# NSA compression: cached tokens transposed by VectorE in 32x32 blocks, from pages fetched in quarters

## What is computed

```python
chunks = kv_pad[:, :, :2].reshape(b, n_chunks, CMP_STRIDE, 2, NSA_KV_HEADS, NSA_HEAD_DIM)   # CMP_STRIDE 16
w1 = w1.reshape(2, CMP_LEN, NSA_HEAD_DIM, CMP_HIDDEN)                                      # 2, 32, 64, 128
pos_bias = jnp.einsum('rld,rlde->re', cmp_pos, w1)
pa = jnp.einsum('bnlrkd,rlde->bnrke', chunks, w1[:, :CMP_STRIDE])
pb = jnp.einsum('bnlrkd,rlde->bnrke', chunks, w1[:, CMP_STRIDE:])
hidden = jax.nn.gelu(pa[:, :-1] + pb[:, 1:] + pos_bias[:, None, :])
out = jnp.einsum('bnrke,ref->bnrkf', hidden, w2)
```

## Time and profile before

| | before |
|---|---|
| median of 3 runs | 2550.19 us (2540.56 to 2556.83) |
| profiled execution, span of the trace | 2552.3 us |
| TensorE busy | 2406.9 us, 94% |
| VectorE busy | 1308.8 us, 51% |
| ScalarE busy | 735.5 us, 29% |
| POOL busy | 26.4 us, 1% |
| share of the 16 DMA engines, SP's queue | 54.8% |

### The profile page before, as it was taken

The page is one execution under the profiler, slowest core; times in us unless marked ns, Lnnn a source line. Parts: engine busy times, 40 slices in busy tenths (PEclk is TensorE's granted clock), DMA queues, the critical chain, the costliest instruction groups (busy, mean ns, idle before and its releaser), DMA issues. The chain is left out here.

```text
span 2552.3 us, 45434 instructions
## 1 busy us (share of the span) xinstructions
PE 2406.9 (94%) x19182; PEld 2040.0 (80%) x19182; DVE 1308.8 (51%) x2332; ACT 735.5 (29%) x1763; POOL 26.4 (1%) x26
## 2 busy tenths in 40 slices
PE   8989988899999889999999898999999998979998
PEld 6668865699986767999888766899985786648998
DVE  2257384265552373666443285366631865535565
ACT  2125373221022342210232293221021445522200
POOL 0000000000000010000000010000000000000000
PEclk9999899999999979999999857999999997889999
DMA  9997616965644317666433255656671865293440
GB/s 346 307 241 166 210 49 214 350 229 213 245 160 144 99 56 283 212 251 223 154 132 134 68 150 195 233 204 256 217 207 66 181 177 159 71 321 122 172 170 22
DMA packets 287343, 472.71 MB, mean 185 GB/s; under 512 B 14956, under 2 KB 105149, under 8 KB 286662
## 3 DMA queue, kind: packets, MB, share of 16 engines
q1 hardware_dynamic: 272370, 456.04, 54.8%
q10 hardware_dynamic: 14770, 13.76, 1.7%
HBM read 448.72 MB, written 38.04 MB: 191 GB/s over the span
## 5 line engine op out<-in xcount | busy, mean ns | idle before, releaser
L631 PE MATMUL PS<-hT,ring 128*128 128x132 f32 x2048 | 249.7, 277 | 6.6 <-DVE hT L756 4.2
L631 PEld LDWEIGHTS PS<-hT,ring 128*128 128x128 f32 x2048 | 238.3, 190 | 11.9 <-issue 11.2
L631 PE MATMUL PS<-mT,arena 128*128 128x132 f32 x1536 | 184.6, 276 | 0.0
L631 PEld LDWEIGHTS PS<-mT,arena 128*128 128x128 f32 x1536 | 178.7, 190 | 0.0
L2687 PE MATMUL PS<-hT,ring 128*128 128x264 f32 x768 | 172.7, 386 | 0.1
L2687 PEld LDWEIGHTS PS<-hT,ring 128*128 128x128 f32 x768 | 145.1, 190 | 24.9 <-issue 0.4
L768 DVE TENSOR_TENSOR arena<-arena,PS 128x264 f32<-128x264 f32 x224 | 89.7, 427 | 130.8 <-PE PS L631 129.6
L715 ACT ACTIVATE arena<-arena 128x528 f32<-128x528 f32 x64 | 41.1, 642 | 312.1 <-DVE arena L768 312.1
L631 PE MATMUL PS<-arena,ring 128*128 128x132 f32 x1024 | 126.9, 277 | 0.0
L631 PE MATMUL PS<-hT,arena 128*128 128x132 f32 x1024 | 125.7, 276 | 0.0
L631 PE MATMUL PS<-mT,ring 128*128 128x132 f32 x1024 | 125.7, 276 | 0.0
(11 more groups left out here) (490 smaller groups left out, 4364.0 us busy)
## 6 DMA issues: line engine op xcount, KB each, us to landing
arena<-in_w_ada SPq DMA_DIRECT2D x36, 2048.0 KB, 12.1
ring<-in_w_mlp_in SPq DMA_DIRECT2D x32, 2048.0 KB, 8.7
ring<-in_w_mlp_out SPq DMA_DIRECT2D x32, 2048.0 KB, 8.1
ring<-in_w_ada SPq DMA_DIRECT2D x12, 2048.0 KB, 19.9
ring<-in_ssd_w_in SPq DMA_DIRECT2D x12, 2048.0 KB, 7.9
ring<-in_nsa_w_in SPq DMA_DIRECT2D x10, 2048.0 KB, 9.5
arena<-in_cache_nsa_kv SPq DMA_DIRECT2D x64, 256.0 KB, 10.5
ring<-in_cache_nsa_kv SPq DMA_DIRECT2D x64, 256.0 KB, 8.0
```

Of the source, the lines that this page charges most:

```text
L631: ins = nc.tensor.matmul(PS[:, bank, at:at + HALF], lhs[:, k, p * 128:(p + 1) * 128], rhs[:, k, :], start=opens and k == 0, stop=closes an ...
```

## The change

The cached tokens are no longer transposed by TensorE through PSUM but by VectorE within SBUF: one instruction transposes 128x1024 numbers in blocks of 32x32 (L1463 in the kernel after). Such a transposition moves numbers only inside a quarter of 32 partitions, so the tokens have to lie in other places. A page is now fetched in four transfers: quarter i takes the tokens 8c + 2i and 8c + 2i + 1 (c from 0 to 15) to the partitions 32i + 16(q mod 2) onwards, 16 neighbouring partitions with two places of 2 KB in each (`quarter_pages`). A group is 64 transfers of 64 KB instead of 16 of 256 KB. SP issues those of 12 pages (48) and POOL those of 4 (16); of group 0 POOL issues all 64, in the input projection and behind the wait for the sample's hidden state (`h_sample`). The buffers are one tile of 16 x 512 numbers a partition each.

The two differences become one instruction of 128x1024 into `delta`, with the odd chunk read twice and the even chunk read at two offsets. The weights lie in the same new order: `w1[0]` and `w1[1]` come in 16 transfers of 32 partitions each (`compress_weights`), and the table of positions in four instead of one. The result of the third product alternates between banks 2 and 4. ScalarE has no copies of cached tokens any more. TensorE's transposes and both copies are gone for all ten products: the prompt's rows go the same way, by four transfers of 32 partitions. The semaphores for transposed data are called `turned` (VectorE done) and `product_made` (TensorE done with `x[:, j]`).

```diff
-            slots = [ring[:, (st["used"] + 2 + i) % SLOTS, :, :] for i in range(2)]
-            return [[P(CMP // 2, 2 * KV * HD) for _ in range(2)], slots]
-
-        def chunk_pages(sp, L, g, G, samples=(0, 1)):
-
-
-            for b in samples:
-                for n in range(0, PAGES, 4):
-                    numbers = page_numbers(sp, [(2 * g + b) * PAGES + q for q in range(n, n + 4)])
-                    for q, number in zip(range(n, n + 4), numbers):
-                        page = cache_chunks[bass.ds(number + L * N_PHYS, 1), :, :, 0:2, :]
-                        fetched[g % 2].on(sp.dma_start(G[g % 2][b][q:128:PAGES],
-                                                       page.rearrange("g c t r n -> (g c) t (r n)")), 16)
+            return [P(2 * PAGES, 2 * KV * HD), ring[:, 0:2].rearrange("p s k n -> p (s k) n")]
+
+        def quarter_pages(engine, kind, signals_, L, g, G, items):
+
+
+            for n in range(0, len(items), 2):
+                b, q0 = items[n]
+                numbers = page_numbers(engine, [(2 * g + b) * PAGES + q for _b, q in items[n:n + 2]], kind)
+                for number, (b, q) in zip(numbers, items[n:n + 2]):
+                    for i in range(4):
+                        part = cache_quarters[bass.ds(number + L * N_PHYS, 1), i, :, :, 0:2, :]
+                        row = 32 * i + 16 * (q % 2)
+                        signals_[g % 2].on(engine.dma_start(G[g % 2][row:row + 16, 8 * b + q // 2 * 2:8 * b + q // 2 * 2 + 2, :],
+                                                            part.rearrange("g c t r n -> (g c) t (r n)")), 16)
+
+        POOL_PAGES = [(1, q) for q in range(4, PAGES)]
+        SYNC_PAGES = [(0, q) for q in range(PAGES)] + [(1, q) for q in range(4)]
+
+        def sync_pages(sp, L, g, G):
+            quarter_pages(sp, mybir.EngineType.SP, fetched, L, g, G, SYNC_PAGES)
+
+        def pool_pages(gp, L, g, G):
+            quarter_pages(gp, mybir.EngineType.Pool, fetched_pool, L, g, G, POOL_PAGES)
+
+        def compress_weights(sp, done, dst, L, r):
+
+            src = a["nsa_cmp_w1"][L, r].rearrange("(h i c d) e -> i d h c e", h=4, i=4, c=4)
+            to = dst.rearrange("p (h c e) -> p h c e", h=4, c=4)
+            for h in range(4):
+                for i in range(4):
+                    done.on(sp.dma_start(to[32 * i:32 * i + 32, h], src[i, :, h]), 16)
...
-                loaded2.on(sp.dma_start(mT_flat[:, 0:2048].rearrange("p (j e) -> p j e", j=16),
-                                        a["nsa_cmp_w1"][L, 0].rearrange("(j p) e -> p j e", p=128)), 16)
-                if first:
-                    chunk_pages(sp, L, 0, G, (0,))
-                    issue(sp, n0 + 11)
-                    chunk_pages(sp, L, 0, G, (1,))
-                    issue(sp, n0 + 13)
-                else:
-                    chunk_pages(sp, L, 0, G)
-                    issue(sp, n0 + 5)
+                compress_weights(sp, loaded2, mT_flat[:, 0:2048], L, 0)
+                issue(sp, n0 + (13 if first else 5))
...
+            def gp_part(gp):
+                gp.wait_ge(h.h_sample.sem, h.h_sample.at(1))
+                quarter_pages(gp, mybir.EngineType.Pool, fetched_pool, L, 0, G, SYNC_PAGES + POOL_PAGES)
...
+            def pair_bank(n):
+
+                return PS[:, (2, 4)[n % 2], 0:256]
...
+            def rows_of(buffer, r, j):
+
+
+                return buffer.rearrange("p (y t) (r k h d) -> p t r h k y d", t=2, r=2, k=KV, h=2)[:, j // 2, r, j % 2]
+
+            def columns_of(j):
+
+
+                return x[:, j, :].rearrange("p (o y q) -> p y q o", o=4, q=8)
+
+            def shifted(j):
+
+
+                y = x[:, j, 0:512]
+                return bass.AP(y.tensor, y.offset, [list(y.ap[0]), [1, 2], [1, 512]])
...
-                    loaded.on(sp.dma_start(w1[1], a["nsa_cmp_w1"][L, 1].rearrange("(j p) e -> p j e", p=128)), 16)
+                    compress_weights(sp, loaded, hT_flat[:, 0:2048], L, 1)
                     loaded2.on(sp.dma_start(w2, a["nsa_cmp_w2"][L].rearrange("r e f -> e r f")), 16)
-                    chunk_pages(sp, L, 1, G)
+                    sync_pages(sp, L, 1, G)
...
-                        sp.wait_ge(pt_ready.sem, pt_ready.at(8 * (g - 1)))
-                        chunk_pages(sp, L, g, G)
+                        sp.wait_ge(turned.sem, turned.at(8 * (g - 1)))
+                        sync_pages(sp, L, g, G)
...
+                @block.gpsimd
+                def _(gp):
+                    for g in (1, 2, 3):
+                        if g > 1:
+                            gp.wait_ge(turned.sem, turned.at(8 * (g - 1)))
+                        pool_pages(gp, L, g, G)
 
...
-                        for b in range(2):
-                            for t in range(2):
-                                for at in range(2):
-                                    o = (2 * t + at) * 128
-                                    c = r * 256 + at * 128
-                                    ins = nc.tensor.transpose(PS[:, 4 + 2 * (m % 2) + b, o:o + R],
-                                                              G[g % 2][b][0:R, 2 * j + t, c:c + 128], ident[0:R, 0:R])
-                        pt_ready.on(ins)
...
-                            nc.tensor.matmul(o[:, 0:256], w1[r][:, j + 4 * u, :], columns(whole(before[:, j, :]), u),
+                            nc.tensor.matmul(o[:, 0:256], w1[r][:, j + 4 * u, :], delta[:, j, 256 * u:256 * u + 256],
...
-                            if n + 1 < len(order):
-                                turn(n + 1, j)
...
+                    def turn(m):
+
+
+                        n, j = divmod(m, 4)
+                        g, r = order[n]
+                        if r == 0 and j == 0:
+                            loaded_group(v, g)
+                        if m >= 4:
+                            v.wait_ge(product_made.sem, product_made.at(m - 3))
+                        if n < cached:
+                            ins = nc.vector.transpose(columns_of(j), rows_of(G[g % 2], r, j))
...
-                        even, odd, y = halves(j)[:, 0], halves(j)[:, 1], whole(after[:, j, :])
-                        nc.vector.tensor_tensor(whole(before[:, j, :]), even, odd, ALU.subtract)
-                        nc.vector.tensor_tensor(chunk_rows(y, 0, 3), chunk_rows(even, 1, 4), chunk_rows(odd, 0, 3), ALU.subtract)
-                        differed.on(nc.vector.tensor_tensor(last_row(y, 3, 0), last_row(even, 0, 1), last_row(odd, 3, 0),
-                                                            ALU.subtract))
+                        v.wait_ge(turned.sem, turned.at(m + 1))
+                        differed.on(nc.vector.tensor_tensor(delta[:, j, :].rearrange("p (a n) -> p a n", a=2), shifted(j),
+                                                            bc(x[:, j, 512:1024], 1, 2), ALU.subtract))
...
-                        for dst, src in regroup(m, 0):
-                            ins = nc.vector.tensor_copy(dst, src)
-                        pt_taken.on(ins)
...
-                            for dst, src in regroup(m, 1):
-                                ins = nc.scalar.activation(dst, src, ACT.Copy)
-                            pt_taken2.on(ins)```

VectorE, compression of layer 0, three turns in the middle of the first products and the end of the second (arena and ring are memory areas in which `x`, `before`, `after`, `delta` and `G` lie; the rows of L1218 and L1233 belong to another piece of work and are only renumbered). Before:

```order
103 L1459 TENSOR_TENSOR ring<-arena 128x8x48
104 L1460 TENSOR_TENSOR ring<-arena 128x8x2x7
105 L1218 SCALAR_TENSOR_TENSOR rstd<-hT,par,rstd 128x128 x4
106 L1479 COPY arena<-PS 64x512 x2
107 L1458 TENSOR_TENSOR ring<-arena 128x512
108 L1459 TENSOR_TENSOR ring<-arena 128x8x48
109 L1460 TENSOR_TENSOR ring<-arena 128x8x2x7
110 L1218 SCALAR_TENSOR_TENSOR rstd<-hT,par,rstd 128x128 x4
111 L1467 TENSOR_TENSOR PS<-PS,arena 128x512
```

193 lines of the change are left out of this document (90 added, 103 removed).

## The result

The changed kernel takes 2595.88 us (median of 4 runs, 2586.53 to 2603.91), the kernel before 2553.51 (4 runs): a ratio of 1.0164, with a 95% interval of 1.0125 to 1.0203. It is slower by 1.6%, where 2540 and no change were forecast, and it lies above the range. The profiled execution is the shortest of the four; its span of 2584.8 us is 32.5 more than before, where the medians differ by 42.

What follows compares the result with a forecast made beforehand. TensorE was taken to set the pace before, page fetching after. Compression savings of 13.8 us, less 2 for POOL's issuing and 2 for delayed weights, gave -10 us: 2540 us as a median, range 2488 to 2592.

Steps and rivals of the forecast that it cites:

- T: Compression stage: time from its start to the last cached product, 129.9 and 130.5 us before, forecast to fall to 123.3.
- The allowance for the projection: Layer 0's input projection: slower page writes may hold back weights while DMA engines are full; 2 us, 0 to 10.
- Rival 3: Input projection: POOL's quarter fetches exceed 1.34 us each and hold the barrier; 2568 us at 1.81; chance 0.12.
- weight stall of 10 us: Layer 0's projection: addition that takes the case of POOL holding the barrier past 2575 us.
- The transfers' rate: Page quarters in the compression: 140 to 160 GB/s expected, 26 to 30 us per group.
- X = 28: Compression: us to fetch one group of pages, from issue (26.1) and transfer (26 to 30) together; break-even 30.3.
- the prediction's own formula: SP's issuing per group: six page pairs of 8 x (t + 0.075) + 0.63, 26.1 us at t = 0.39; T = 39.3 + 3X.
- T = 123.3: Compression: 39.3 + 3X at X = 28, three groups fetched one after another; 6.6 and 7.2 us saved.
- 22.4 + 2: End of the compression: 22.4 us for the last group, 2 for VectorE's transpose and difference before its first product.
- The transpose: VectorE's 128x1024 transpose in the compression: 1.22 us taken, bounded above by 2.7; VectorE's turn 2.6 us.
- rival 4: Compression: a slow transpose of 2.7 us makes VectorE's turn 4.1 and T 139; +18 us, 2568; chance 0.06.
- TensorE's side: Compression: transposes gone, 28 us less per layer; 2.6 us of matmuls a turn, 2.8 with a quarter output product.

Runs made afterwards that it cites:

- pacing: Changed kernel, but in layer 0 POOL fetches only two pages of group 0 after each projection product from the eighth on; 1.0081 of the kernel before.
- the run with all fetching undone: Changed kernel with whole pages to every eighth partition, group 0 by SP at its old places, w1 in one transfer each; 0.9874 of the kernel before.
- the run on the transpose's steps: Changed kernel with contiguous or stepped reads and writes tried in four turns of the cached groups' transposes, half writing contiguously; one run, 2602.82 us.

## Why the prediction was wrong

Two steps of the prediction failed, and they weigh about the same. The two projections were given 4 us in the sum and cost 27 (29.25 in layer 0, -2.0 in layer 3). T was to save 13.8 us in both layers and lost 12.4, a miss of 26.

- **The allowance for the projection (2 us, 0 to 10).** It measured 24.4 us by S, and 24 to 31 with the scatter of S (29.3 by the start). The prediction asked whether POOL would be done before the block's end, and it was, 93 us early: 64 quarters in 43 us, 0.67 us each with the register work (0.504 for the transfer alone), half of the 1.34 allowed. It should have asked what 4.19 MB issued from 53 us on do to the ring, whose weights were all needed in order and came through engines that were full already, as the earlier trace rows showed. Before, SP's own order kept pages and weights apart. The runs show a cost of 21 us for a block of spread pages on POOL's queue, the neighbours' low rate on top, and 13 to 15 us still with pacing. Rival 3, POOL holding the barrier, fell; its "weight stall of 10 us" was the right thing at less than half its size.
- **The transfers' rate.** 140 to 160 GB/s was expected for quarters: 141 to 154 GB/s were measured in three windows of the compression while pages came (230 to 254, 262 to 275, 276 to 288 us). Right.
- **X = 28** was right by number: 27.4, 27.7 and 28.3. By the prediction's own formula it was luck. The issue of a quarter was 0.317 us, below the lower bound of 0.333, and with it the formula gives 22.6. But two pages took 27.44 / 6 = 4.57 us, which is 2.04 more than their eight issues, where the formula has 8 x 0.075 + 0.63 = 1.23: what lies between the issues was priced too low. The two errors cancelled.
- **T = 123.3 measured 134.7 and 138.1.** By SP's rows in layer 0: head 8.9 (10.5 forecast), group 1 27.4, group 2 from 38.2 to 66.0, then SP idle for 5.2 us, since VectorE freed group 1's buffer only at 260.13; group 3 28.3; landing 3.0; and 32.1 from there to the last product, where 22.4 + 2 stood. Two terms were wrong: the 5.2 (the formula had SP never idle) and 7.7 at the end. By the rows, both are waits between VectorE and TensorE, which the formula put at nothing: VectorE's list holds pieces that TensorE needs behind transposes of the next group. No run moves these pieces.
  - *The 5.2.* VectorE needed from 229.91 to 259.46 for group 1's eight transposes, and 6.44 us of that it stood for TensorE, which had itself stood 10.67 us for the copy of L1447 and restarted at half clock. Without it the buffer would have been free at 253.0 (an estimate), before SP was done with group 2 at 254.9. The stand is in every version with the new computing, and not for the pages: in the run with all fetching undone, where VectorE never waits for one, it is 6.64 us. The slower transpose adds to it (8 x 0.72 = 5.8 us of VectorE's time, an estimate), but shorter transposes did not remove the idle time: with half of them at 1.22, in the run on the transpose's steps, SP stood idle for 8.5 us.
  - *The 7.7.* TensorE ended the stage, not VectorE:

```profile
294.53 1.22 PE L1399 MATMUL PS<-ring,hT 128*128 128x256 f32 x2 [4.45 <-DVE ring L1474]
...
322.04 1.03 PE L1409 MATMUL PS<-arena,ring 128*128 128x256 f32 x4
```

  The last difference of group 2 (L1474) is queued behind the first transpose of group 3, which waited for its pages until 291.49. So when they had landed TensorE had nine turns to do and not eight, from 294.53 on without a wait: the first took 5.3 us at a granted clock of 0.50, the others 2.6 each, with two output products between them. VectorE's last difference was done 6.2 us before SP's next transfer. Of the transpose's 1.94 us only 0.72 is in this term.
- **The transpose.** The value 1.22 rested on "steps in SBUF have cost nothing". L2261's steps were no measure of a write with 1024 bytes between neighbours. VectorE's turn was 2.93 us and a fourth of 0.59, a group 24.6, for 20.8 forecast without the output product. The upper bound of 2.7 held. It makes VectorE the busiest engine, as in rival 4, but how much of T it costs no run separates.
- **TensorE's side** was right in part: its passes took 2.6 us a turn at the full clock, but over the stage the granted clock was 0.84 to 0.86 because of its waits, and it set the end. The extra POOL issue, positions and barrier cost nothing measurable, and layer 3's projection, with DMA engines to spare, lost nothing (-2.0 us).

That a whole page, spread and issued by SP at its old places, would have kept the gain is shown by the run with all fetching undone. The 13 to 15 us that remain under pacing are the DMA engines' lower rate; how much of that comes from the 16 neighbours and how much from a second queue was not separated, since no run paces spread pages.

## What to carry to other kernels

When transfers move to another queue, look at what the old queue's order protected: all queues end in the same DMA engines, which served them here packet by packet in turn, and a block of prefetches that is issued early delays the weights that are needed now. Price a transfer by its destination too; quarters to 16 neighbouring partitions were cheap to issue and expensive to carry. Look also for small pieces that another engine needs and that stand in a list behind an instruction that can wait. And a layout that serves a 32x32 transpose has a step somewhere; find out which of writer and readers pays it before counting on the contiguous time.

## What the runs showed of the hardware

- A quarter of a page to every eighth partition costs SP 0.557 us of issue where one to 16 neighbours costs 0.317; a whole page costs 0.539 and 0.564. On POOL quarters cost 0.503 and 0.504, whole pages 0.529 and 0.532.
- Three DMA queues with work were served with equal numbers of packets: 877, 879 and 876 in 20 us; SP's then moved 89 GB/s.
- With full DMA engines, 285 and 255 GB/s to spread partitions fell to 213 and 159 GB/s to neighbours.
- VectorE's 32x32 transpose of 128x1024 takes 1.22 to 1.25 us with contiguous writes and 1.94 to 1.97 with writes 1024 bytes apart; a subtraction of the same size 1.21 and, read at every fourth number, 1.95.
- TensorE's 256-column pass took 0.26 us with contiguous moving numbers and 0.49 with every fourth one.
